# The order of two-head and one-head units in a streaming encoder's first mixer

## The reference, cut to what matters

```python
def ab_mixer(xn, w_in, w_out, lower_bound, a_gnorm, w_gk, b_gk, b_gnorm, s_a, s_b):
    h = jnp.einsum('btd,de->bte', xn, w_in)
    a_q, a_f, a_i, a_g, b_q, b_k, b_v, b_g, b_lr = split_cols(h, AB_SIZES)
    f = lower_bound + (1.0 - lower_bound) * jax.nn.sigmoid(a_f)
    o_a, s_a_new = gated_linear_recurrence(silu(a_q), 1.0 - f, a_i, log(f), s_a)      # 4 heads, key width 128
    o_a = rmsnorm(o_a, a_gnorm) * silu(a_g)
    gk = b_lr @ w_gk + b_gk
    log_alpha = log_sigmoid(gk) / 16
    o_b, s_b_new = gated_linear_recurrence(b_q / 8, b_k, b_v, log_alpha, s_b)         # 4 heads, key width 64
    o_b = rmsnorm(o_b, b_gnorm) * silu(b_g)
    return concatenate([o_a, o_b]) @ w_out, s_a_new, s_b_new
```

## Time and profile before

| what | us |
|---|---|
| median of 3 runs | 1434.17 (1433.86 to 1434.9) |
| the profiled execution | 1434.03 |
| its span | 1432.3 |
| TensorE matmuls busy | 1395.0 (97% of the span) |
| VectorE busy | 576.6 (40%) |
| ScalarE busy | 557.7 (39%) |
| GpSimd busy | 589.0 (41%) |

### The profile page before, as it was taken

One profiled execution on the slowest core, in us unless ns is written; L12 is line 12 of the kernel. 1 busy time (PEld: TensorE's weight loads), 2 busy tenths in 40 slices (PEclk: granted clock), 3 DMA queues, 4 the chain that ended last, 5 costly groups with the idle time before them and its releaser, 6 DMA issues.

```text
span 1432.3 us, 27287 instructions
## 1 busy us (share of the span) xinstructions
PE 1395.0 (97%) x11038; PEld 1318.2 (92%) x11038; DVE 576.6 (40%) x1068; ACT 557.7 (39%) x907; POOL 589.0 (41%) x303
## 2 busy tenths in 40 slices
PE   8999999899999999999999999999999999999997
PEld 6788899799999999999989878877999999999997
DVE  6615556424421233122324976664633113311234
ACT  5634655434432243212345344443543223421222
POOL 4332122143544344434444556564244524453442
PEclk9999999899999999999999999999999999999999
DMA  5221222143323222322242322101133323332221
GB/s 179 75 74 49 58 70 64 38 129 89 88 86 106 66 85 86 115 60 76 82 115 72 89 76 76 52 27 35 46 103 88 103 74 88 87 104 69 82 70 62
DMA packets 204486, 114.34 MB, mean 80 GB/s; under 512 B 16500, under 2 KB 198648, under 8 KB 204408
## 3 DMA queue, kind: packets, MB, share of 16 engines
q1 hardware_dynamic: 199056, 109.47, 26.4%
q10 hardware_dynamic: 5352, 3.76, 0.8%
HBM read 107.26 MB, written 5.96 MB: 79 GB/s over the span
## 4 chain that ended last, share of the span: by engine, by line
PE 70%; issue 21%; POOL 6%; DVE 1%; ACT 1%; POOLq 0%; DVEq 0%; ACTq 0%
PE ps L1137 56%; POOL w_lo L590 6%; PE ps L1326 3%; PE ps L1272 3%; PE ps L1638 1%; PE ps L1287 1%; PE ps L1594 1%; PE ps L1606 1%; PE ps L1336 0%; PE ps L1630 0%; DVE small L2189 0%; PE ps L1523 0%; ACT arena L960 0%; PE ps L1569 0%; DVE arena L2307 0%
## 5 line engine op out<-in xcount | busy, mean ns | idle before, releaser
L590 POOL TENSOR_TENSOR w_lo<-w_raw,w_hi 128x1024 fp32r<-128x1024 f32 x202 | 499.6, 2477 | 734.0 <-ACT w_hi L655 734.0
L1137 PE MATMUL ps<-x_hi,w_hi 128*128 128x272 f32 (+1 forms) x1840 | 383.7, 290 | 5.9 <-POOL w_lo L590 3.2
L1137 PE MATMUL ps<-x_hi,w_lo 128*128 128x272 f32 (+1 forms) x1840 | 380.7, 288 | 0.0
L1137 PE MATMUL ps<-x_lo,w_hi 128*128 128x272 f32 (+1 forms) x1840 | 379.4, 288 | 0.0
L1137 PEld LDWEIGHTS ps<-x_hi,w_hi 128*128 128x128 f32 (+1 forms) x1840 | 287.7, 187 | 12.6 <-issue 6.1
L1137 PEld LDWEIGHTS ps<-x_lo,w_hi 128*128 128x128 f32 (+1 forms) x1840 | 288.1, 188 | 0.5
L1137 PEld LDWEIGHTS ps<-x_hi,w_lo 128*128 128x128 f32 (+1 forms) x1840 | 286.3, 188 | 0.5
L655 ACT ACTIVATE w_hi<-w_raw 128x1024 fp32r<-128x1024 f32 x202 | 211.3, 1050 | 156.2 <-PE ps L1137 126.6
L1137 PE MATMUL ps<-o_hi,w_hi 128*128 128x272 f32 x832 | 173.4, 290 | 1.3 <-DVE arena L2023 1.1
L1137 PE MATMUL ps<-o_hi,w_lo 128*128 128x272 f32 x832 | 173.0, 289 | 0.0
L1137 PE MATMUL ps<-o_lo,w_hi 128*128 128x272 f32 x832 | 172.4, 289 | 0.0
(11 more groups left out here) (310 smaller groups left out, 1747.9 us busy)
## 6 DMA issues: line engine op xcount, KB each, us to landing
w_raw<-in_ffn_w_in SPq DMA_DIRECT2D x88, 512.0 KB, 3.8
w_raw<-in_ffn_w_out SPq DMA_DIRECT2D x32, 512.0 KB, 3.7
w_raw<-in_ab_w_in SPq DMA_DIRECT2D x28, 512.0 KB, 3.7
w_raw<-in_cd_w_in SPq DMA_DIRECT2D x13, 512.0 KB, 3.7
w_raw<-in_ffn_w_out SPq DMA_DIRECT2D x16, 384.0 KB, 3.3
w_raw<-in_ab_w_out SPq DMA_DIRECT2D x8, 512.0 KB, 4.1
arena<-in_x_prompt SPq DMA_DIRECT2D x4, 512.0 KB, 5.4
w_raw<-in_cd_w_in SPq DMA_DIRECT2D x8, 256.0 KB, 3.8
```

Source lines behind the costliest of these rows:

```text
L590: pool.tensor_tensor(wl[:, s, :], raw[:, s, :], wh[:, s, :].bitcast(F32), ALU.subtract).then_inc(lo_done, 1)
L1137: mm = pe.matmul(ps[0:M, b + h, 0:HALF], w[:, s, k * M:(k + 1) * M], xs[x][:, k, h * HALF:(h + 1) * HALF], start=(begin and k == ks[0] and ...
```

## The change

The list of units is written out in another order. Everything that is worked out from it (weight chunks, jobs, semaphore counts, the loops of every engine) follows.

```diff
-    units = [("b", t) for t in range(BH // 2)] + [("a", u) for u in range(AH)]
+    units = [("b", 0), ("a", 0), ("a", 1), ("b", 1), ("a", 2), ("a", 3)]
+    assert len(units) == BH // 2 + AH
     NU = len(units)
```

## The result

The new order is slower: 1439.08 us (median of nine runs, 1436.66 to 1443.61) against 1434.90 (nine runs, 1433.86 to 1435.75), a ratio of 1.0031 with a 95% interval of 1.0021 to 1.0040: 4.4 us by the ratio, 4.2 between the medians. The forecast was 1433.8 with no difference that can be measured, its range 1432.3 to 1436.0. Not only the middle moved: the runs of the new order lie 7 us apart, those of the old one 2 us (later sets of runs of the old kernel lie 4 us apart, see e4).

A forecast was written before the change was run, and what follows sets the result against it. TensorE was taken to bound the kernel. Rounds of 38.98 + 26.71 + 27.85 + 38.98 + 26.75 = 159.27 us, less 159.70, gave -0.43; 1434.17 - 0.4 = 1433.8 us, range 1432.3 to 1436.0.

The forecast's parts named there:

- The frame: First mixer's unit rounds: a reorder keeps the same matmuls and saves at most TensorE's waits, 3.4 to 3.6 us.
- rounds 4 and 5: Two-head to one-head, then one-head to one-head handovers: forecast like rounds already seen, 38.98 and 26.75 us.
- the sum: Five handover rounds in the new order: 159.27 us less 159.70, so -0.43 us, or 0 if VectorE's pause returns.
- The one new round: Round 3, one-head to two-head handover: no new TensorE wait, 1.10 us more for gate matmuls, 27.85 us in all.
- The rounds that only move: Rounds 1, 2, 4 and 5: taken as like rounds seen, 38.98, 26.71, 38.98 and 26.75 us.
- Rival (b): One-head to two-head handover: a PE gap of 1.5 us or more brings the clock down, 1440.3 us; chance 0.04.
- The sign of a clock below 1.00: Any round ahead of the tail: a granted clock below 1.00 would show the forecast wrong.
- The signs for a wait: New round: TensorE waiting over 0.3 us at L1444 or the key job would show the forecast wrong.
- rival (d): Two-head units: their own waits vanish if neighbours mattered, saving 3.2 us, to 1431.0 us; chance 0.03.
- Rival (a): New round at L1914: GpSimd comes first, adding 1.5 us of TensorE wait, 1435.3 us; chance 0.08.
- The pause of VectorE: Old round 4, amid the states: a 0.46 us pause, 0.40 of the forecast gain; likely covered elsewhere, or may return.

The follow-up runs named there:

- e4: Changed kernel with two edits, ScalarE copying the later two-head unit's key out of PSUM early and the sigmoid table loaded early: 1434.89 us, ratio 1.0003 to the old kernel.
- e2: Changed kernel with ScalarE copying the key of two-head units but the first out of PSUM as soon as its job is done: 1435.70 us, ratio 1.0013.
- e5: Old kernel's unit list reordered to two, one, one, one, two, one heads: 1439.09 us, ratio 1.0029 to the old kernel.
- e6: Old kernel's unit list reordered to two, one, two, one, one, one heads: 1439.36 us, ratio 1.0036 to the old kernel.
- e3: Changed kernel with one tiny extra sigmoid loading the table ahead of ScalarE's wait for the first one-head key job: 1439.39 us, ratio 1.0031.
- e1: Changed kernel run again without further edits: 1438.93 us, ratio 1.0033 to the old kernel.
- e8: Changed kernel plus eight unread 128x128 matmuls behind round 3's outputs, where TensorE otherwise waits 2.25 us: 1436.59 us, ratio 1.0022 to the old kernel.
- e7: Old kernel run again, unedited, for a second profile: 1434.05 us.
- e9: Old kernel plus sixteen unread 128x128 matmuls behind the last round's outputs, where TensorE waits 4.67 us: 1433.87 us, ratio 0.9999.

## Why the prediction was wrong

**The frame held.** That the change can only move waits of TensorE, that rounds 4 and 5 are like those seen, that the two-head rounds keep their own waits (1.01 and 0.6 us each), that the new round's extra matmuls cost 1.10 us, and that the tail's wait stays 4.67: all are in the profile. e4 gives the sum to 0.1 us.

**The step that failed first** is "The one new round", where the prediction checked the pairs for the gate matmuls and for the key job, and stopped there: the gate job of that round, the third user of a pair, was never checked. Before the change the prediction said of the second one-head unit's gate only that it and its turned outputs "still follow the jobs that free them". It follows the key job of a two-head unit, and that job's pair is freed by L1944 and not by a sigmoid. The trace of before had what was needed to price it: VectorE's decays end, ScalarE's exponentials follow, and L1943 began 1.61 us after VectorE's last instruction. The term that it put at nothing measured 2.25 us: round 3 took 31.54 us in place of 27.85, with 2.25 of waiting and some 1.6 by the clock; e4's, without both, took 27.71. e2 shows the cause, e5 and e6 its place.

**The second step** is in "The rounds that only move": round 1 "becomes two-one: it was seen at 38.98", with the sigmoid at no cost. The round that was seen had the sigmoid's table loaded already, by the gate of the round before. Behind the first unit there is none, and the load of 1.28 us, which the prediction did count for the new round, is not hidden by the wait ahead of it here. Measured: 0.92 us; e3 shows the cause.

**The clock.** Rival (b) said that a wait at this handover could bring the clock down, gave it 0.04, and priced it at 5 us after the tail's 10 us. The handover was right, though the wait there was the gate job's and not the one for the running states that (b) priced at 1.5 us; the size of the fall was not: 3.4 us at half clock, 1.7 us. The argument against it, that gaps of 1.0 us did nothing, does not reach to a gap of 2.25. That matmuls on few rows can be followed by a fall without any wait was not in the prediction. Of the 4.8 us between the means of e1 and before, 2.5 are waits by the table's last column (3.2 by the timelines), at most 2.2 the clock.

**Signs and bounds.** The sign of a clock below 1.00 in a round ahead of the tail came true in rounds 2 and 3. The signs for a wait named L1444 and the key job of the new round, and neither waited there: the gate job was missing from this list as it was from the sum. In the range, 1435.3 and a spread of 1 us make 1436.3 and not 1436.0, and the 1431.0 of rival (d) counts from 1434.17 where the others count from 1433.8; neither changes the outcome.

**Rival (a)**, GpSimd ahead of VectorE in the new round, did not come about, by a still smaller margin than forecast. Timelines of DVE and of POOL:

```profile
174.66 0.72 DVE L1915 TENSOR_TENSOR arena<-arena 128x544 f32<-128x544 f32 x1
```

```profile
174.76 2.84 POOL L591 TENSOR_TENSOR w_lo<-w_raw,w_hi 128x1024 fp32r<-128x1024 f32 x1 [3.17 <-ACT w_hi L656]
```

VectorE came first by 0.10 us and GpSimd took 2.84 us for the usual 2.4. The Trainium skill tells of an exclusive port that the two share in "Trainium Architecture — The Big Picture", "What this means for kernel authors"; the 0.44 us more agree with it. The pause of VectorE, of which the sum hoped to be rid, came back elsewhere, as the prediction allowed.

## What to carry to other kernels

When an order is changed, go down the list of buffers in rotation and ask of *every* user at the new border who frees what it takes over, and when; two kinds of work that look alike may give their buffer back at opposite ends of their chain. Ask the same of state that an engine carries from one piece of work to the next, such as a loaded function table: a piece that was cheap in its old place had a predecessor that paid for it. And when TensorE is the bound, price a new wait with the clock: here taking out a wait of 2.25 us gave back 3.2 us in the medians of e1 and e2, and 2.25 + 1.7 us by the timelines.

## What the runs showed of the hardware

A wait of 2.25 us behind the small matmuls of the outputs was followed by 3.4 us at 1.2 GHz in all five profiles that had it (changed, e1, e3, e5, e6), beginning between 0.2 us ahead of its end (e3) and 1.4 us behind it (e1), and at that place in none of the three without it or with it filled (e2, e4, e8). Waits of 1.01 us were never followed by one in these profiles; one of 1.5 us at 56 us, ahead of the rounds, was in e7 and not in the others. Matmuls on 32, 64 or 16 of the 128 rows were at times followed by one too, with no wait ahead (148.1 in the changed kernel, 271.1 in e3, 174.7 in e5, 100.9 in e7), at other times not, in the same kernel. Outside the rounds five of the twelve profiles (e1, e2, e3, e6, e9) have such a stretch that begins between 924 and 934 us, TensorE being busy throughout it, and the others have none there. Whether the same work brings the clock down thus differs from run to run; the nine runs of the changed kernel lie 7 us apart, with mean clocks from 0.994 down to 0.988. What decides it was not tried. The Trainium skill says in "TensorE: Matmul & The Clock Gate", "What's actually happening", that the monitor behind the gate runs freely and does not start anew with a kernel; the differing places agree with that but do not show it.

A table load of ScalarE can lie in the wait ahead of its instruction or behind it. In the changed kernel's round 1 L804 loaded at 111.34 and L794 at 115.83, inside their waits (their instructions began at 115.19 and 119.47); L779, which has two waits ahead of it, loaded behind 7.02 us of idle time. Why the one differs from the others was not tried apart; e3 shows only that a tiny instruction of the same table ahead of the waits moves the load out.
